# A mixer loop whose recurrence steps stand 2.5 slots apart instead of 2, with the gated norm partly on ScalarE and keys rounded once

## What is computed

```python
# gated linear attention, 8 heads of 64, forward and backward over the tokens
S, o = scan: A = einsum(q, k, decay);  o = (q * exp(b)) @ S + A @ v
             S = exp(b_last) * S + (k * exp(b_last - b))^T @ v
og = rmsnorm(o_f + o_b, gla_norm) * silu(gg)
# windowed attention: 8 query heads, 2 key heads, 128 local tokens each side + 512 cached context keys, sink logit
p = softmax_with_sink(concat(s_loc, s_ctx));  osw = p @ concat(v_loc, v_ctx)
x = x + g1 * (concat(og, osw) @ w_o)
x = x + g2 * (square(relu(h @ w_ff1)) @ w_ff2)
```

## Time and profile before

| | |
|---|---|
| median of 3 runs | 1687.52 us (1684.58 to 1689.86) |
| the profiled execution, its own time | 1684.21 us |
| its span from first to last instruction | 1682.3 us |
| TensorE busy | 1603.9 us, 95% |
| VectorE busy | 1020.3 us, 61% |
| GpSimd busy | 1016.3 us, 60% |
| ScalarE busy | 673.6 us, 40% |
| mean granted TensorE clock | 0.993 |

### The profile page before, as it was taken

The page is one execution under the profiler, slowest core; times in us unless marked ns, Lnnn a source line. Parts: engine busy times, 40 slices in busy tenths (PEclk is TensorE's granted clock), DMA queues, the critical chain, the costliest instruction groups (busy, mean ns, idle before and its releaser), DMA issues.

```text
span 1682.3 us, 31906 instructions
## 1 busy us (share of the span) xinstructions
PE 1603.9 (95%) x11618; PEld 1394.7 (83%) x11618; DVE 1020.3 (61%) x1584; ACT 673.6 (40%) x1192; POOL 1016.3 (60%) x758
## 2 busy tenths in 40 slices
PE   4999999998999888899999999999999999999997
PEld 1998778996777766788888998989978899998996
DVE  2713565666676669455866566575695545545468
ACT  2514224225444345312354444444535444444441
POOL 1711554654574789002487787777898667667682
PEclk9999999999999999999999999999999999999999
DMA  9254565659555455333661322313235132231322
GB/s 331 92 159 137 196 210 175 224 179 263 160 171 158 158 158 152 108 130 142 200 224 57 100 75 75 100 51 99 88 114 174 51 100 72 78 100 50 99 64 100
DMA packets 211450, 225.93 MB, mean 134 GB/s; under 512 B 52752, under 2 KB 171664, under 8 KB 208144
## 3 DMA queue, kind: packets, MB, share of 16 engines
q1 hardware_dynamic: 209248, 224.46, 41.6%
q10 hardware_dynamic: 2096, 0.02, 0.1%
HBM read 177.22 MB, written 47.24 MB: 133 GB/s over the span
## 4 chain that ended last, share of the span: by engine, by line
PE 43%; POOL 4%; DVE 2%; issue 1%; ACT 0%; DMA 0%; SPq 0%; DVEq 0%; ACTq 0%; POOLq 0%
PE ff_banks L3095 8%; PE ff_banks L3096 8%; PE ff_banks L3097 8%; PE ff_banks L3068 7%; PE ff_banks L3070 7%; PE ff_banks L3069 7%; POOL h_whi L2734 1%; POOL h_xop L2332 1%; POOL h_wlo L2746 1%; POOL h_whi L2741 1%; DVE ff_tmp L2935 1%; DVE ff_acc L2925 0%; DMA ff_hb<-in_w_ff 0%; DVE ff_acc L2919 0%; DVE ff_acc L2892 0%
## 5 line engine op out<-in xcount | busy, mean ns | idle before, releaser
L3068 PE MATMUL ff_banks<-h_xop,h_whi 128*128 128x320 f32 x888 | 275.2, 310 | 5.8 <-DVE wo_raw L2872 3.1
L3070 PE MATMUL ff_banks<-h_xop,h_whi 128*128 128x320 f32 x888 | 274.4, 309 | 0.0
L3069 PE MATMUL ff_banks<-h_xop,h_whi 128*128 128x320 f32 x888 | 274.4, 309 | 0.0
L2892 DVE TENSOR_TENSOR ff_acc<-ff_acc,ff_banks 128x512 f32<-128x512 f32 x294 | 199.0, 681 | 99.2 <-PE ff_banks L3097 99.2
L3095 PE MATMUL ff_banks<-h_wlo 128*128 128x512 f32 x600 | 234.3, 390 | 1.6 <-DVE ff_acc L2892 0.8
L3097 PE MATMUL ff_banks<-h_wlo 128*128 128x512 f32 x600 | 233.5, 389 | 0.0
L2734 POOL TENSOR_TENSOR h_whi<-mid_raw,h_whi 128x512 fp32r<-128x512 f32 x149 | 207.2, 1406 | 1.4 <-ACT h_whi L2586 1.4
L2746 POOL TENSOR_TENSOR h_wlo<-mid_raw,h_wlo 128x320 fp32r<-128x320 f32 x128 | 116.6, 913 | 129.6 <-ACT mid_raw L2623 129.6
L3068 PEld LDWEIGHTS ff_banks<-h_xop,h_whi 128*128 128x128 f32 x888 | 166.7, 188 | 9.5 <-issue 4.8
L3069 PEld LDWEIGHTS ff_banks<-h_xop,h_whi 128*128 128x128 f32 x888 | 166.7, 188 | 1.1
L3070 PEld LDWEIGHTS ff_banks<-h_xop,h_whi 128*128 128x128 f32 x888 | 166.7, 188 | 0.0
(11 more groups left out here) (306 smaller groups left out, 3774.2 us busy)
## 6 DMA issues: line engine op xcount, KB each, us to landing
mid_raw<-in_w_ff SPq DMA_DIRECT2D x124, 512.0 KB, 4.3
mid_raw<-in_w_ada SPq DMA_DIRECT2D x18, 1024.0 KB, 7.2
early_room<-qk_by_channel SPq DMA_DIRECT2D x20, 512.0 KB, 4.1
proj<-prj_stage SPq DMA_DIRECT2D x60, 152.0 KB, 1.9
mid_raw<-in_w_in SPq DMA_DIRECT2D x6, 1216.0 KB, 7.2
early_room<-in_w_ada SPq DMA_DIRECT2D x6, 1024.0 KB, 10.9
decays<-early_room SPq DMA_DIRECT2D x8, 640.0 KB, 4.5
early_room<-decays SPq DMA_DIRECT2D x20, 256.0 KB, 2.9
```

What stands on the lines that cost most here:

```text
L2892: dve.tensor_tensor(acc[:, p, at], acc[:, p, at], down[n % RING], ALU.add).then_inc(added, 1)
L3068: pe.matmul(out, w_hi[:, k], x_hi[:, k], start=(k == 0), stop=False)
L3069: pe.matmul(out, w_hi[:, k], x_lo[:, k], start=False, stop=False)
L3070: mm = pe.matmul(out, w_lo[:, k], x_hi[:, k], start=False, stop=(k == KH - 1))
```

## The change

It has six parts, all inside `mixer` and its helpers. (1) Recurrence steps stand 2.5 slots apart (0, 2, 5, 7, ... 40), their second halves one slot later, the last at 41 instead of 33; the glo tiles 2 to 9 go to slots 28 to 46 instead of 24 to 46, the wo blocks to 44 to 53 instead of 37 to 50. (2) TensorE's order in a slot: the first place of preparation goes ahead of the scores, the recurrence's transposes are split off and stand right behind the scores, and the recurrence's scores stand ahead of the values. ScalarE's and VectorE's orders follow. (3) Of the glo norm, the addition of 1 and the square go from GpSimd to ScalarE; glo loads are issued two slots ahead in place of one, ScalarE's part comes one slot later, VectorE's sum at the start of the slot after that, GpSimd's second half two slots after the first. (4) The state update of both partition halves is written to the same PSUM columns, so that VectorE scales it in one instruction instead of two. (5) The keys are rounded once, into `khl`, and `kdup` is gone. (6) `glo_o` has two buffers, and semaphore counts follow.

```diff
@@ GlaOutput
-        pool.tensor_tensor(self.sq[:, :], self.o[:, :], self.o[:, :], ALU.mult).then_inc(self.sq_ready, 1)
-        pool.wait_ge(self.tanh_ready, n + 1)
-        pool.tensor_tensor(self.factor[:, :], self.tanh[:, j], self.one[:, 0:1].broadcast_to([P, GW]), ALU.add).then_inc(self.factor_ready, 1)
-        pool.wait_ge(self.factor_ready, n + 1)
-        pool.tensor_tensor(self.si[:, :], self.gg[:, j], self.factor[:, :], ALU.mult).then_inc(self.si_ready, 1)
+        act.activation(self.tanh[:, :], self.gg[:, n % 2], ACT.Tanh, scale=0.5).then_inc(self.tanh_ready, 1)
+        act.wait_ge(self.tanh_ready, n + 1)
+        act.activation(self.factor[:, n % 2], self.tanh[:, :], ACT.Identity, bias=1.0).then_inc(self.factor_ready, 1)
+
+    def act_square(self, act, n):
+        act.wait_ge(self.o_ready, n + 1)
+        if n:
+            act.wait_ge(self.ssq_ready, n)
+        act.activation(self.sq[:, :], self.o[:, n % 2], ACT.Square).then_inc(self.sq_ready, 1)
...
     def pool_scale(self, pool, n):
         j = n % 2
+        pool.wait_ge(self.factor_ready, n + 1)
+        if n:
+            pool.wait_ge(self.out_ready, n)
+        pool.tensor_tensor(self.si[:, :], self.gg[:, j], self.factor[:, j], ALU.mult).then_inc(self.si_ready, 1)
         pool.wait_ge(self.ssq_ready, n + 1)
@@ Recurrence
-    def pe_scores(self, pe, x):
+    def pe_turned(self, pe, x):
...
-            pe.wait_ge(self.new_ready, 2 * x)
+            pe.wait_ge(self.new_ready, x)
         for b in range(self.HP):
             tr = pe.transpose(self.ps[:, 2, b * P:(b + 1) * P], self.ke[:, d, b], self.keep["ident"])
         tr.then_inc(self.tr_ready, 1)
+
+    def pe_scores(self, pe, x):
...
-                mm = pe.matmul(self.ps[rows, 2, c:c + DH], self.kt[:, d, c:c + DH], self.v[:, j, c:c + DH], start=True, stop=True)
+                mm = pe.matmul(self.ps[rows, 2, b * DH:(b + 1) * DH], self.kt[:, d, c:c + DH], self.v[:, j, c:c + DH], start=True, stop=True)
...
-        for half in range(2):
-            rows = slice(half * DH, (half + 1) * DH)
-            upd = self.ps[rows, 2].rearrange("p (b c) -> p b c", c=P)[:, :, half * DH:(half + 1) * DH]
-            dve.tensor_tensor(self.new[rows], upd, self.decayed(d, t, rows, 2), ALU.mult).then_inc(self.new_ready, 1)
+        dve.tensor_tensor(self.new[:, :, :], self.update(), self.decayed(d, t, slice(0, P), 2), ALU.mult).then_inc(self.new_ready, 1)
@@ Keys
-        act.activation(self.keys_of(self.kdup, slice(0, P), n), self.turned(slice(0, P), n), ACT.Copy).then_inc(self.dup_ready, 1)
-        act.activation(self.keys_of(self.khl, slice(0, DH), n), self.turned(slice(0, DH), n), ACT.Copy).then_inc(self.hl_ready, 1)
+        act.activation(self.keys_of(self.khl, slice(0, P), n), self.turned(slice(0, P), n), ACT.Copy).then_inc(self.hl_ready, 1)
@@ mixer
-        scores_at = {2 * (x - FIRST): x for x in range(FIRST, X)}
-        outputs_at = {2 * (x - FIRST) + 1: x for x in range(FIRST, X)}
+        scores_at = {5 * (x - FIRST) // 2: x for x in range(FIRST, X)}
+        outputs_at = {5 * (x - FIRST) // 2 + 1: x for x in range(FIRST, X)}
         GLO_ORDER = [0, 1, 5, 6, 4, 7, 3, 8, 2, 9]
-        glo_at = dict(zip((5, 8, 24, 27, 30, 33, 36, 39, 42, 46), range(NT)))
-        wo_at = dict(zip((37, 38, 40, 41, 44, 45, 48, 50), range(D // P)))
+        glo_at = dict(zip((5, 8, 28, 30, 33, 35, 38, 40, 43, 46), range(NT)))
+        wo_at = dict(zip((44, 45, 47, 48, 50, 51, 52, 53), range(D // P)))
@@ mixer, SyncE
-                    if w + 1 in glo_at:
-                        n = glo_at[w + 1]
+                    if w + 2 in glo_at:
+                        n = glo_at[w + 2]
@@ mixer, GpSimd
-                    if w - 1 in glo_at:
-                        glo.pool_scale(pool, glo_at[w - 1])
+                    if w - 2 in glo_at:
+                        glo.pool_scale(pool, glo_at[w - 2])
@@ mixer, TensorE
+                    ahead((w, 0))
                     if w < SLOTS:
                         scores(2 * w)
                         scores(2 * w + 1)
-                    ahead((w, 0))
+                    if w in scores_at:
+                        rec.pe_turned(pe, scores_at[w])
+                    ahead((w, 1))
                     late = 1 <= w <= SLOTS and crossing(w)
+                    if w in scores_at and not late:
+                        rec.pe_scores(pe, scores_at[w])
...
-                    ahead((w, 1))
-                    if w and w in scores_at:
+                    if w in scores_at and late:
                         rec.pe_scores(pe, scores_at[w])
@@ mixer, ScalarE
-                    if w in glo_at:
-                        glo.act(act, glo_at[w])
+                    if w - 1 in glo_at:
+                        glo.act(act, glo_at[w - 1])
+                        glo.act_square(act, glo_at[w - 1])
@@ mixer, VectorE
+                    if w - 2 in glo_at:
+                        glo.dve(dve, glo_at[w - 2])
                     ahead((w, 0))
                     ahead((w, 1))
...
-                    if w - 1 in glo_at:
-                        glo.dve(dve, glo_at[w - 1])
```

79 lines of the change are left out of this document (36 added, 43 removed).

## The result

| | before | after |
|---|---|---|
| median of 4 runs | 1686.6 us | 1700.6 us (1699.5 to 1702.3) |
| ratio, 95% interval | 1 | 1.0082 (1.0062 to 1.0101) |
| the profiled execution, its own time | 1684.2 us | 1702.3 us |
| its span | 1682.3 us | 1700.5 us |
| mean granted TensorE clock | 0.993 | 0.979 |

The time is above the range that was given (1672 to 1688). The two profiled executions lie 18.1 us apart, the medians 14.0, so sums over their rows come out somewhat large. A ratio is always taken against runs of the kernel before on the same chip; their median lay between 1686.5 and 1688.7 us.

A forecast was written before the change was run, and what follows sets the result against it. TensorE bounds the loop to about slot 24, GpSimd from there to the last glo tile. GpSimd's earlier end gives -8, wo blocks cost 1: -7 from 1684.2 is 1677.2, plus 3.3 for the median 1680.5 us; range 1672 to 1688.

The forecast's parts named there:

- The sum at the head of VectorE's slot: Glo norm: sum taken a slot ahead of GpSimd's use, saving 2.7 us of GpSimd's waits; VectorE's wait there gone.
- Steps 2.5 slots apart: Slots 0 to 23 lose 8.1 us, slots 24 to 27 2.4; GpSimd's shorter tiles give 1.3 and 1.6 more.
- GpSimd as the bound behind slot 24: From slot 28 GpSimd sets the pace: tile 8.34 us, over 85% busy, ending at 667.1 in place of 675.6 us.
- Loads and the clock: In the loop, ScalarE's four waits for glo loads, 15.6 us, go; costed at nothing, at most 15.6 us.
- Keys and merged update: Ahead of the loop: 0.2 us for the keys' start, 1.3 us for merged scaling; term -1.5, ends 0 and -4.
- Slower: ScalarE, held by GpSimd at the square, stops TensorE beyond about 5.5 us of wait: +9, 1696.5 us; chance 0.10.
- Both tests that the text gave for a wrong mechanism: TensorE's idle time behind slot 28 below 8 us, or ScalarE several times over 5 us at the square, TensorE with it.
- TensorE alone: TensorE is the only bound; moved steps fill its idle time in slots 28 to 41: -15, 1672.5 us; chance 0.15.
- No gain: Behind slot 24 GpSimd's lag passes on through new places, standing some 5 us more: -2, 1685.5 us; chance 0.25.

The follow-up runs named there:

- the small edits alone: Kernel before with only the keys rounded once and the state update scaled in one VectorE instruction: 1687.8 us, ratio 0.9996.
- the twin with the sum in the middle: Full change with VectorE's sum of squares moved from the head of its slot to between the preparation places and the recurrence's mask: 1688.0 us, ratio 1.0005.

## Why the prediction was wrong

**The sum at the head of VectorE's slot.** This is the step that failed. The text took 2.7 us of GpSimd's waits for the sum as saved, since the sum "is now taken a slot ahead of GpSimd's use", and expected that "the wait of VectorE for the square at the sum of squares is gone". Whom it waits for in its new place, and what is queued behind it, was never worked out. It waits 27.9 us, GpSimd's waits for the sum grew from 2.7 to 6.1 us, and that place alone is worth +0.77%, 13 us. The earlier trace rows had the mechanism in them: a 2.32 us wait there, and then 2.77 us of TensorE's. With the sum in the middle the change stands at 1688.0 us, level with the kernel before and still 7.5 above the forecast; the steps below are the rest.

**TensorE's new order** had no term. By itself it costs 0.4% (1.0036 against 0.9996), some 7 us, about 4 of them by query copies that wait for scores behind them; on top of the spacing it is 0.1% (1.0021 to 1.0032), within the intervals.

**Steps 2.5 slots apart.** The removal was right, though the change itself hid it (its slot 24 opened 2.6 us earlier, not 11): in the kernel with the spacing alone slots 0 to 27 took 145.7 us in place of 157.8 with the small edits alone (12.1 less, forecast 8.1 + 1.3 + 2.4 + 1.6 = 13.4), and slot 28 of the twin with the sum in the middle opened at 559.8 us (forecast 560.6). What was wrong is where the moved work lands. Slots 28 to 41 became 10.2 us longer (83.7 against 73.5), with TensorE busy for 13.6 us more: only 3.4 us of the moved steps fell into idle time. The forecast let GpSimd hide them.

**GpSimd as the bound behind slot 24.** The tile was sized rightly (584.42 to 591.42 us and the sum's 1.27 give 8.3 us, forecast 8.34). But the stage did not follow it. In slots 28 to 41 with the wider spacing and the old order, GpSimd had 75.7 us to do in 83.7 with its old norm, and 63.5 in 85.8 with 12 us taken off it and the sum in the middle: no shorter. TensorE was busy for 75 us in both. After the change it was busy for 63.64 of 87.70 us there, 73% and not 85%, and the last tile ended at 687.9 us, not at 667.1. GpSimd was late there because its input came late. The loads of the slot-30 tile stand in SyncE's queue behind a step's output and the next step's loads and are issued at 575.8 to 579.3 us, so that the sum waits for them; three such waits are 16.0 us:

```profile
583.19 1.27 POOL L1086 TENSOR_TENSOR mix_glo_o<-mid_raw 128x512 f32<-128x512 f32 x1 [6.79 <-DMA mid_raw<-proj]
```

**Loads and the clock.** ScalarE's waits for glo loads went as forecast, at no gain; they moved to GpSimd (8.6 us before, 16.0 after). The clock was assumed unchanged; it gave 8.5 of the 17.8 us. The "about 21 us" that the text counted as not TensorE's are 23.8 us of idle time and 3.6 of lower clock by its own rows; no term rests on them.

**Keys and merged update.** The merged instruction took 0.42 us, as taken; the term of -1.5 us did not show (0.9996, 0.9980 to 1.0012; slot 0 opened at 417.65 us in place of 416.88).

**The rivals.** *Slower* (0.10) was right in its sign, and its engine too: ScalarE's square. But its mechanism, ScalarE held by GpSimd, was 4.3 us after the change. It is real where it passes the bound that was named (6.61 us against some 5.5), and costs TensorE 4.82 us once in the twin. The price came from VectorE standing where ScalarE was to stand. Both tests that the text gave for a wrong mechanism missed: TensorE's idle time behind slot 28 is 22.3 us (16.9 before), not below 8, and ScalarE never stood longer than 1.6 us at the square; the test that would have caught it was VectorE's waits, on which the text was sure. *TensorE alone* (0.15) was right that GpSimd is not the bound behind slot 24, and wrong that the moved steps would fill idle time. *No gain* (0.25) is nearest to what the spacing alone measured (1690.2 us, where it said 1685.5), by another path than the one that it named.

**The parts add up along one path**: small edits 0.9996; with spacing and order 1.0032; with the norm split and its sum in the middle 1.0005; with the sum at the head 1.0082. The norm's part (-0.27%) is the same without spacing and order (0.9996 to 0.9969). Spacing and order are not so independent: with the norm in and the sum in the middle, spacing costs 0.5% (0.9969 to 1.0023), and the order then gives back some 0.2% (1.0023 to 1.0005, with intervals that touch). Whether and why the order helps there stays open.

**The best kernel** is the one without spacing and order: norm split between GpSimd and ScalarE, sum between preparation and mask, update merged, keys rounded once. It takes 1681.5 us, 0.31% less than before (0.9954 to 0.9983) and 1.1% less than the change.

## What to carry to other kernels

When an instruction moves to the head of an in-order engine's slot, price its wait by the time at which its input is made, and everything queued behind it; a 0.7 us instruction cost 13 us here. A wait is nearly free as long as the engine would have stood anyway, so an edit that lets other inputs come earlier (the new order) can make an old wait dear: test placement and order together, and the sum's place by itself. And where work is moved off a stage that TensorE fills, show first which idle time of TensorE takes it in.

## What was not expected of the hardware

The granted clock makes short waits dearer than they are. Around slot 8 two waits of TensorE, 2.33 and 1.04 us, delayed that slot by 3.6 us, and slots 8 to 11 then ran at a granted clock of 0.81 and took 4.1 us more for the same 315 matmuls with no more idle time. A mean of 0.81 is one of the two levels, 2.4 GHz, for some 62% of these 26.8 us and the other, 1.2 GHz, for 38%, 10.2 us. The Trainium skill, TensorE: Matmul & The Clock Gate, section "HAM oscillation — how this bites in real kernels", counts half of the throttled time as lost. By that, as an estimate, it would be 5.1 us; the rows show 24.61 - 19.91 = 4.7 us of slower matmuls, so the trace agrees.

The other thing is the price of a stop on VectorE. 38.8 us of it cost 29 to 30 us on an engine that was busy for 194 of the loop's 277 us: in this loop of dependent steps across four engines, free time on one of them was not room.
